# Start addresses of the on-chip operands of a 1-core transformer kernel: multiples of 128 bytes

## Chip, cores and metric

The kernel runs on 1 core of one Trainium2 chip. The metric is the device time of one execution in microseconds. TensorE has two clock levels, 1.2 and 2.4 GHz.

## What is computed

Three blocks one after the other on an activation `x` of 256 tokens by 1024 features, all in 4-byte floats. Each layer is a residual sum of feed-forward parts and one mixer:

```python
# first block, 2 layers (mixers: compressed/selected/window attention, then window attention)
x = x + 0.5 * swiglu(rmsnorm(x, ffn1_norm[i]), ffn1_w_gu[i], ffn1_w_down[i])   # D_FF = 2816
h = rmsnorm(x, mix_norm[i])
x = x + mixer(h)
x = x + 0.5 * swiglu(rmsnorm(x, ffn2_norm[i]), ffn2_w_gu[i], ffn2_w_down[i])
# second block, 1 layer: the same frame with shift, scale and gate made from c_2 @ w_ada_2
# third block, 4 layers (stick-breaking attention, short convolution, gated linear attention, stick-breaking)
h = h + rms_norm(m, norm_gains[i, 1])
f = jnp.square(jax.nn.relu(rms_norm(h, norm_gains[i, 2]) @ w_up)) @ w_down      # D_FF_3 = 4096
h = h + rms_norm(f, norm_gains[i, 3])
```

There are 6 gated feed-forward layers (silu) and 4 ReLU ones.

## The kernel before

**Split products.** Every large product is made of rounded operands (type F32R). A value is split into a rounded high part and the rest: ScalarE copies `raw` to `hi` (`split_hi`, L329), VectorE subtracts, `lo = raw - hi` (`split_lo`, L336). A product is then hi·hi + hi·lo + lo·hi, three matmuls added up in PSUM.

**Operands on chip.** Weights arrive in `ring_in` (units of 2048 columns, 1 MB) and `ring_down`, two slots each, and are split into `in_hi`, `in_lo` and `down_hi`, `down_lo`. Activations that enter a product lie transposed in `feat` (both parts in one tensor, `feat_hi` and `feat_lo`, 8 chunks of 256 tokens). Where a mixer's output projection comes just before, they lie in `feat2_hi` and `feat2_lo` instead, at the end of the arena (class `Feed`). The hidden values of a feed-forward unit are split into `hid_hi` and `hid_lo`; `act` holds them unsplit. `hyb_hi` and `hyb_lo` are activations of the second block's mixer.

**Feed-forward (class `FeedForward`).** TensorE turns over units: hidden(i), down(i-1), hidden(i+1), down(i). A unit of a gated layer is 128 gate and 128 up columns, 22 units; `_chunk` (L1099 to L1101) issues 16 x 3 matmuls of 256 columns, weights stationary and `feat` (or `feat2`) streamed. Its down projection (`_down_block`, L1169 to L1171) issues 4 x 3 matmuls of 512 columns, `hid` stationary, `down_hi` and `down_lo` streamed. A unit of a ReLU layer is 256 columns, 16 units; `_chunk` issues 16 pairs, one of 512 columns that streams `feat_hi` and `feat_lo` in two parts of 256 (L1097), one of 256 (L1098), and 24 down matmuls. ScalarE and VectorE split the next unit's weights meanwhile, and make the hidden values of this one.

**Mixer projections.** `Linear` (L1455 to L1457) and its kin (L4020 to L4022, L3816 to L3818) hold 128 tokens of features stationary and stream 512 columns of `in_hi` or `in_lo`. Others (L1985 to L1987, L3359 to L3361, L3996 to L3998) hold weights and stream 256 columns of `feat`. L1846 is a matmul of the stick-breaking attention on unsplit 4-byte operands of the arena.

**Modulation.** Three of the gated layers (the two `ffn1` and the second `ffn2` of the first block) have GpSimd work beside them that adds up `c_2 @ w_ada_2` from `mod_w` into `mod_sum`. The order on each engine is that of a list of stages; waits are semaphores written by hand.

**Placement.** `Core.__init__` allocates the tensors one after another, each from the current `nc.sbuf_base`. `ring_down`, `hid_hi` and `hid_lo` share the space of `proj`; `down_hi`, `down_lo`, `mod_sum`, `mod_w`, `feat2`, `hyb` and some masks share that of `arena`. The start bytes within a partition in the built program, and what is left over 128:

| tensor | before | over 128 | after | over 128 |
|---|---|---|---|---|
| const | 16512 | 0 | 16512 | 0 |
| x / y | 31584 / 39776 | 96 | same | 96 |
| feat | 47968 | 96 | 48000 | 0 |
| in_hi / in_lo / ring_in | 64352 / 80736 / 97120 | 96 | 64384 / 80768 / 97152 | 0 |
| act | 113504 | 96 | 113536 | 0 |
| proj, ring_down | 123040 | 32 | 123136 | 0 |
| hid_hi / hid_lo | 139424 / 143520 | 32 | 139520 / 143616 | 0 |
| arena, down_hi | 147744 | 32 | 147840 | 0 |
| down_lo | 164128 | 32 | 164224 | 0 |
| feat2_hi / feat2_lo | 205088 / 213280 | 32 | 205184 / 213376 | 0 |
| hyb_lo / hyb_hi | 199296 / 214304 | 0 / 32 | 199392 / 214400 | 96 / 0 |

Of the kernel before, what the change touches and what calls it, by code (L numbers as in the profile page):

```python
# [116 lines left out]
    return slice(n * BLK, (n + 1) * BLK)  # L117

class Signal:  # L120

# [15 lines left out]
class Core:  # L138

    def __init__(self, nc, ctx, dram):
        self.nc, self.dram = nc, dram

        def sb(name, *shape):
            return ctx.enter_context(nc.sbuf_tensor(name, [P, *shape], F32))
# [4 lines left out]
        def split(name, *shape):  # L150
            return ctx.enter_context(nc.sbuf_tensor(name, [P, *shape], F32R))

        self.sb, self.sig = sb, sig
        self.const = sb("const", CONST_N)
        self.cols = sb("cols", COL_N)
        self.x = sb("x", TT, D)
        self.y = sb("y", TT, D)

        self.feat = split("feat", 2, KC, TOKENS)
        self.feat_hi, self.feat_lo = self.feat[:, 0], self.feat[:, 1]  # L160
        self.in_hi = split("in_hi", RING, UNIT)
        self.in_lo = split("in_lo", RING, UNIT)
        self.ring_in = sb("ring_in", RING, UNIT)
# [3 lines left out]
        self.fold = sb("fold", TT, P)  # L167
        self.minus_half = sb("minus_half", 8)
        self.eps = sb("eps", 8)
        at = nc.sbuf_base  # L170
        self.proj = sb("proj", TT, PROJ_COLS)

        def placed(name, offset, dtype, *shape):
            return nc.alloc_sbuf_tensor_at(name, [P, *shape], dtype, offset=offset)
# [3 lines left out]
        self.hid_hi = placed("hid_hi", at, F32R, RING, 2 * TOKENS)  # L179
        at += 4 * RING * 2 * TOKENS  # L180
        self.hid_lo = placed("hid_lo", at, F32R, RING, 2 * TOKENS)
        at = nc.sbuf_base
        self.arena = sb("arena", ARENA)
        self.down_hi = placed("down_hi", at, F32R, RING, UNIT)
# [6 lines left out]
        at = nc.sbuf_base - 4 * 2 * KC * TOKENS  # L191
# [4332 lines left out]
```

## Time and profile before

| | |
|---|---|
| three timed runs, us | 2889.39, 2891.58, 2892.72 (median 2891.58) |
| profiled execution, span | 2889.2 us (the page gives this execution by its span alone) |
| busy: TensorE / VectorE / ScalarE / GpSimd | 96% / 66% / 42% / 21% |
| mean granted TensorE clock | 0.986 |
| DMA | 173 GB/s mean, 500 MB |

The busy share of an engine is the time in which some instruction of it runs. Matmuls are pipelined: the next one starts before the last has ended, so a matmul's printed duration isn't what it costs; the distance between two starts is. PE is TensorE, PEld its loading of stationary values, DVE is VectorE, ACT ScalarE, POOL GpSimd, SP the queue that issues DMAs. The names right of the arrow are the operands, the streamed one first, then the stationary one; `feat_hi` and `feat_lo` stand there for `feat2`, `feat` for both parts of `feat`. In `128*128 128x512`, the first is the rows and columns of the array that are used, the second the output.

### The profile page before, as it was taken

How to read it: one execution, taken by the hardware profiler on the slowest of the kernel's cores; microseconds unless marked ns; L12 is line 12 of the kernel's file. 1: busy time of each engine (PE TensorE's matmuls, PEld its weight loads, DVE VectorE, ACT ScalarE, POOL GpSimd, SP SyncE). 2: the span in 40 equal slices, each digit the busy share in tenths (PEclk: the TensorE clock that was granted, in tenths of full speed). 3: DMA queues.
4: the chain of work that ended last, by engine and by line, in shares of the span. 5: the costliest groups of instructions: out<-in, count | busy, mean ns of one | idle time of the engine just before them, and what ended most of it. 6: DMA issues, size and time to landing. Idle time of an engine off the chain costs nothing.

```text
span 2889.2 us, 43862 instructions
## 1 busy us (share of the span) xinstructions
PE 2775.3 (96%) x17408; PEld 2446.4 (85%) x17408; DVE 1903.6 (66%) x2046; ACT 1201.3 (42%) x1478; POOL 609.9 (21%) x510
## 2 busy tenths in 40 slices
PE   8999999999989999999899999999899989999998
PEld 7997789999878988988699897888788878888887
DVE  6985656688867885555655556666666657655665
ACT  4343443343444334334444345334433444435433
POOL 6953300068434861000100000000000320000000
PEclk9999999999999999999999999999999999999999
DMA  7745134557526664443355434544554345533542
GB/s 278 265 183 163 45 145 189 186 215 275 184 73 225 254 241 175 180 147 103 110 184 186 146 132 178 196 157 160 194 195 163 118 145 197 197 126 116 211 187 103
DMA packets 126466, 500.31 MB, mean 173 GB/s; under 512 B 11025, under 2 KB 12337, under 8 KB 92961
## 3 DMA queue, kind: packets, MB, share of 16 engines
q1 hardware_dynamic: 112768, 450.39, 42.8%
q0 software_dynamic: 13600, 48.60, 4.9%
q8 instruction: 65, 1.06, 0.2%
q14 instruction: 33, 0.26, 0.0%
HBM read 497.90 MB, written 1.05 MB: 173 GB/s over the span
## 4 chain that ended last, share of the span: by engine, by line
PE 74%; DVE 13%; issue 6%; ACT 3%; POOL 2%; DMA 1%; DVEq 0%; SPq 0%; ACTq 0%; POOLq 0%
PE duo L1097 7%; PE duo L1169 7%; PE duo L1170 7%; PE duo L1171 7%; PE duo L1099 6%; PE duo L1100 6%; PE duo L1101 6%; PE duo L1098 4%; DVE down_lo L336 3%; PE duo L1455 3%; PE duo L1457 3%; PE duo L1456 3%; DVE in_lo L336 3%; ACT in_hi L329 2%; DVE hid_hi L1279 1%
## 5 line engine op out<-in xcount | busy, mean ns | idle before, releaser
L336 DVE TENSOR_TENSOR in_lo<-ring_in,in_hi 128x2048 fp32r<-128x2048 f32 x296 | 706.5, 2387 | 306.1 <-ACT in_hi L329 305.9
L329 ACT CAST in_hi<-ring_in 128x2048 fp32r<-128x2048 f32 (+1 forms) x293 | 554.5, 1893 | 276.8 <-PE duo L1457 152.3
L1169 PE MATMUL duo<-down_hi,hid_hi 128*128 128x512 f32 x1040 | 412.4, 397 | 10.9 <-DVE hid_lo L1281 7.5
L1170 PE MATMUL duo<-down_lo,hid_hi 128*128 128x512 f32 x1040 | 409.7, 394 | 0.0
L1171 PE MATMUL duo<-down_hi,hid_lo 128*128 128x512 f32 x1040 | 409.5, 394 | 0.0
L1099 PE MATMUL duo<-feat,in_hi 128*128 128x256 f32 x1408 | 400.1, 284 | 6.5 <-DVE in_lo L336 6.1
L1100 PE MATMUL duo<-feat,in_hi 128*128 128x256 f32 x1408 | 399.3, 284 | 0.0
L1101 PE MATMUL duo<-feat,in_lo 128*128 128x256 f32 x1408 | 399.1, 283 | 0.0
L336 DVE TENSOR_TENSOR down_lo<-ring_down,down_hi 128x1024 fp32r<-128x1024 f32 (+1 forms) x196 | 373.1, 1904 | 34.4 <-ACT down_hi L329 34.4
L1097 PE MATMUL duo<-feat,in_hi 128*128 128x512 f32 x1024 | 360.4, 395 | 0.0
L329 ACT CAST down_hi<-ring_down 128x1024 fp32r<-128x1024 f32 (+1 forms) x196 | 260.2, 1328 | 73.3 <-PE duo L1171 72.1
L1098 PE MATMUL duo<-feat,in_lo 128*128 128x256 f32 x1024 | 284.3, 278 | 0.0
L1099 PEld LDWEIGHTS duo<-feat,in_hi 128*128 128x128 f32 x1408 | 270.5, 192 | 11.2 <-DVE in_lo L336 6.1
L1100 PEld LDWEIGHTS duo<-feat,in_hi 128*128 128x128 f32 x1408 | 270.9, 192 | 3.2
L1101 PEld LDWEIGHTS duo<-feat,in_lo 128*128 128x128 f32 x1408 | 270.8, 192 | 0.0
L1169 PEld LDWEIGHTS duo<-down_hi,hid_hi 128*128 128x128 f32 x1040 | 196.0, 188 | 55.8 <-issue 16.0
L1171 PEld LDWEIGHTS duo<-down_hi,hid_lo 128*128 128x128 f32 x1040 | 195.7, 188 | 45.8
L1097 PEld LDWEIGHTS duo<-feat,in_hi 128*128 128x128 f32 x1024 | 192.0, 188 | 45.6 <-DVE in_lo L336 0.5
L1170 PEld LDWEIGHTS duo<-down_lo,hid_hi 128*128 128x128 f32 x1040 | 196.1, 189 | 37.2
L908 POOL TENSOR_TENSOR small<-small,minus_half 128x1 f32<-128x1 f32 x16 | 8.9, 554 | 1024.6 <-DVE small L941 1024.3
L3122 POOL TENSOR_TENSOR mod_sum<-mod_sum,mod_w 128x1024 f32<-128x1024 f32 x63 | 210.1, 3335 | 5.3
L1219 ACT ACTIVATE act<-act 128x256 f32<-128x256 f32 x88 | 36.8, 418 | 416.9 <-DVE act L1269 416.9
(487 smaller groups left out, 5286.0 us busy)
## 6 DMA issues: line engine op xcount, KB each, us to landing
ring_in<-in_ffn_in SPq DMA_DIRECT2D x196, 1024.0 KB, 6.4
ring_down<-in_ffn_down SPq DMA_DIRECT2D x132, 512.0 KB, 3.5
ring_down<-in_ffn_down SPq DMA_DIRECT2D x64, 1024.0 KB, 4.8
mod_w<-in_w_ada POOLq DMA_DIRECT2D x72, 512.0 KB, 5.2
ring_in<-in_sb_w_qkv SPq DMA_DIRECT2D x24, 1024.0 KB, 5.1
ring_in<-in_conv_w_in SPq DMA_DIRECT2D x12, 1024.0 KB, 5.2
ring_in<-in_gla_w_in SPq DMA_DIRECT2D x12, 1024.0 KB, 5.1
ring_in<-in_nsa_w_in SPq DMA_DIRECT2D x10, 1024.0 KB, 5.3
```

What stands on the lines that cost most here:

```text
L329: act.copy(hi[:, s, 0:n], raw[:, s, 0:n]).then_inc(hi_ready.sem, 1)
L336: dve.tensor_tensor(lo[:, s, 0:n], raw[:, s, 0:n], hi[:, s, 0:n].bitcast(F32), ALU.subtract).then_inc(lo_ready.sem, 1)
L1097: pe.matmul(out.rearrange("p (s n) -> p s n", s=2), hi, k.feat[:, :, c, :], start=c == 0, stop=False, skip_group_check=True)
L1098: return pe.matmul(out[:, 0:TOKENS], lo, k.feat_hi[:, c, :], start=False, stop=(c == KC - 1), skip_group_check=True)
L1099: pe.matmul(out, hi, self.feat_hi[:, c, :], start=opens, stop=False, skip_group_check=True)
L1100: pe.matmul(out, hi, self.feat_lo[:, c, :], start=False, stop=False, skip_group_check=True)
L1101: return pe.matmul(out, lo, self.feat_hi[:, c, :], start=False, stop=(c == KC - 1), skip_group_check=True)
L1169: pe.matmul(out, k.hid_hi[:, j, rows], k.down_hi[:, s, cols], start=opens, stop=False)
L1170: pe.matmul(out, k.hid_hi[:, j, rows], k.down_lo[:, s, cols], start=False, stop=False)
L1171: return pe.matmul(out, k.hid_lo[:, j, rows], k.down_hi[:, s, cols], start=False, stop=closes)
L1455: pe.matmul(out, f_hi, w_hi[:, c, :], start=(h == 0 and c == 0), stop=False)
L3122: pool.tensor_tensor(total, total, mod.w[:, s, :], ALU.add).then_inc(mod.used.sem, 1)
```

## The change

Four constants of phases, all 0, and a helper that allocates a gap tensor up to the wanted phase. Two of the gaps exist in the built program (32 bytes before `feat`, 64 before `proj`); the other two are empty. Nothing else is touched: each engine issues the same instructions in the same order, with other addresses.

```diff
+LINE = 128
+FEATURE_PHASE, WEIGHT_PHASE, HIDDEN_PHASE, ARENA_PHASE = 0, 0, 0, 0
...
+        def phase(name, at):
+            gap = (at - nc.sbuf_base) % LINE
+            if gap:
+                sb(name, gap // 4)
...
+        phase("feature_gap", FEATURE_PHASE)
         self.feat = split("feat", 2, KC, TOKENS)
         self.feat_hi, self.feat_lo = self.feat[:, 0], self.feat[:, 1]
+        phase("weight_gap", WEIGHT_PHASE)
         self.in_hi = split("in_hi", RING, UNIT)
         self.in_lo = split("in_lo", RING, UNIT)
...
         self.eps = sb("eps", 8)
+        phase("hidden_gap", HIDDEN_PHASE)
         at = nc.sbuf_base
         self.proj = sb("proj", TT, PROJ_COLS)
...
         self.hid_lo = placed("hid_lo", at, F32R, RING, 2 * TOKENS)
+        phase("arena_gap", ARENA_PHASE)
         at = nc.sbuf_base
         self.arena = sb("arena", ARENA)
```

## Rows read from the trace of the kernel before

**Rows 1.** Page, sections 1 and 4: busy time per engine; the chain that ended last.

```profile
PE 2775.3 (96%) x17408; PEld 2446.4 (85%) x17408; DVE 1903.6 (66%) x2046; ACT 1201.3 (42%) x1478; POOL 609.9 (21%) x510
...
PE 74%; DVE 13%; issue 6%; ACT 3%; POOL 2%; DMA 1%; DVEq 0%; SPq 0%; ACTq 0%; POOLq 0%
```

**Rows 2.** Groups by line and form, TensorE: busy us, mean ns, idle before.

```profile
L1169 PE MATMUL duo<-down_hi,hid_hi 128*128 128x512 f32 x1040 | 412.4, 397 | 10.9 <-DVE hid_lo L1281 7.5 <-DVE hid_lo L1296 3.1
...
L1099 PE MATMUL duo<-feat,in_hi 128*128 128x256 f32 x1408 | 400.1, 284 | 6.5 <-DVE in_lo L336 6.1 <-DVE feat L615 0.5
...
L1097 PE MATMUL duo<-feat,in_hi 128*128 128x512 f32 x1024 | 360.4, 395 | 0.0
...
L1099 PE MATMUL duo<-feat_hi,in_hi 128*128 128x256 f32 x704 | 196.2, 279 | 0.1
...
L1455 PE MATMUL duo<-in_hi,feat 128*128 128x512 f32 x432 | 172.5, 399 | 3.7 <-DVE in_lo L336 3.6
...
L1985 PE MATMUL duo<-feat,in_hi 128*128 128x256 f32 x256 | 72.6, 284 | 0.0
```

**Rows 3.** Timeline, TensorE: start us, us, instruction; gated layer, `feat` streamed.

```profile
1479.75 0.28 PE L1099 MATMUL duo<-feat,in_hi 128*128 128x256 f32 x1
...
1481.43 0.28 PE L1101 MATMUL duo<-feat,in_lo 128*128 128x256 f32 x1
```

**Rows 4.** Timeline, TensorE; gated layer, `feat2_hi` and `feat2_lo` streamed.

```profile
449.65 0.28 PE L1099 MATMUL duo<-feat_hi,in_hi 128*128 128x256 f32 x1
...
451.69 0.28 PE L1099 MATMUL duo<-feat_hi,in_hi 128*128 128x256 f32 x1
```

**Rows 5.** Timeline, TensorE; down projection, split down weights streamed.

```profile
1490.43 0.40 PE L1169 MATMUL duo<-down_hi,hid_hi 128*128 128x512 f32 x1
...
1493.22 0.28 PE L1099 MATMUL duo<-feat,in_hi 128*128 128x256 f32 x1
```

**Rows 6.** Timeline, TensorE; ReLU layer, two-part stream, then one part.

```profile
1858.22 0.40 PE L1097 MATMUL duo<-feat,in_hi 128*128 128x512 f32 x1
...
1861.69 0.40 PE L1097 MATMUL duo<-feat,in_hi 128*128 128x512 f32 x1
```

**Rows 7.** Timeline, TensorE; mixer projection, `in_hi` and `in_lo` streamed.

```profile
252.26 0.40 PE L1455 MATMUL duo<-in_hi,feat 128*128 128x512 f32 x1
...
254.99 0.39 PE L1455 MATMUL duo<-in_hi,feat 128*128 128x512 f32 x1
```

**Rows 8.** Timeline, TensorE; before 22 us, the same stream as rows 3.

```profile
21.00 0.41 PE L1099 MATMUL duo<-feat,in_hi 128*128 128x256 f32 x1
...
21.64 0.41 PE L1099 MATMUL duo<-feat,in_hi 128*128 128x256 f32 x1
```

**Rows 9.** Timeline, and line L1846 alone: unsplit 4-byte operands.

```profile
1718.69 0.60 PE L1846 MATMUL duo<-arena,const 128*128 128x256 f32 x2
...
L1846 PE MATMUL duo<-arena,const x64: 378/379/483, 1708.1 to 2671.2; 128*128 128x256 f32 x64
```

**Rows 10.** Stretches of single layers: us, then each engine's busy us, clock, DMA.

```profile
53.20:206.60 153.40, 153.40 (x1073) 143.43 (x1071) 135.56 (x112) 58.64 (x55) 120.20 (x64) 1.00 0.66 244
...
920.90:1078.70 157.80, 152.50 (x1081) 141.18 (x1080) 138.81 (x114) 59.23 (x55) 123.23 (x66) 1.00 0.70 256
```

**Rows 11.** Waits of VectorE, 53.2 to 206.6 us: us in total, times, longest.

```profile
DVE act L1274 <- ACT act L1219: 8.7, 18, 0.5
DVE in_lo L336 <- ACT in_hi L329: 4.1, 5, 1.1
```

**Rows 12.** Timeline, TensorE; `in_hi`, `in_lo` streamed against `hyb_hi`, `hyb_lo`.

```profile
1407.28 0.39 PE L3816 MATMUL duo<-in_hi,hyb_hi 128*128 128x512 f32 x1
...
1409.34 0.39 PE L3816 MATMUL duo<-in_hi,hyb_hi 128*128 128x512 f32 x1
```

**Rows 13.** Groups of VectorE, 1824 to 1924 us (a ReLU layer).

```profile
L336 DVE TENSOR_TENSOR in_lo<-ring_in,in_hi 128x2048 fp32r<-128x2048 f32 x10 | 22.9, 2292 | 11.1 <-ACT in_hi L329 11.1
L336 DVE TENSOR_TENSOR down_lo<-ring_down,down_hi 128x2048 fp32r<-128x2048 f32 x9 | 20.6, 2292 | 6.1 <-ACT down_hi L329 6.1
```

## Prediction

> **What bounds the kernel now.** I read the page first. TensorE is busy 96% of the span, and the chain that ended last lies on it for 74% and on VectorE for 13% [rows 1]. So the kernel is bound by the rate of its matmuls, and a view of waits can tell little; next come the groups by line. Nearly all matmuls there are of the split kind (rounded 4-byte operands, three products for one), in few shapes: a stream of 512 or of 256 columns against 128x128 stationary values [rows 2]. The printed durations (about 395 and 280 ns) overlap, since matmuls are pipelined; what a matmul costs is the distance from its start to the next one's. That I take from the timeline, over many in a row.
>
> In a gated layer that streams `feat`, 14 steps take 1481.43 - 1479.75 = 1.68 us: 120.0 ns for 256 columns [rows 3]. In a gated layer that streams `feat2_hi` and `feat2_lo`, the same line with the same weight buffers, 18 steps take 2.04 us: 113.3 ns [rows 4]. At 2.4 GHz and one column a cycle it would be 106.7 ns. So the same shape has two prices, 13.3 and 6.7 ns above the ideal. What differs is where the stream starts: `feat` 96 bytes past a multiple of 128, `feat2` 32 bytes past one. The other streams are all off a multiple too. Down projection (32 past): 12 steps in 2.79 us, 232.5 ns for 512 columns, where the ideal is 213.3 [rows 5]. ReLU layer (96 past): 10 pairs of a 512- and a 256-column step in 3.47 us, 347 ns a pair against 320 [rows 6]. Mixer projection (96 past): 12 steps in 2.73 us, 227.5 ns [rows 7].
>
> **The change, part by part.** No instruction, wait or transfer is added, removed or reordered. From `feat` to `eps` everything moves up by 32 bytes, from `proj` on by 96. Every full-rate stream then starts on a multiple of 128, since its inner offsets are multiples of 512.
>
> The price of an aligned step lies between the ideal (106.7 and 213.3 ns) and today's 120 and 232 (above, should it get worse: the rival on the other side). I take 109 and 216: the ideal plus the 2 ns that the stream without visible excess shows [rows 9]. The terms:
> - ReLU layers, 4 with 16 units each. A unit has 16 pairs, (347 - 325) x 16 = 0.35 us, and 24 down steps, (232 - 216) x 24 = 0.38 us. 64 x 0.73 = **47 us**. They hold the 1024 steps of L1097 [rows 2]. VectorE waits there for ScalarE, and ScalarE for TensorE, so there is room [rows 13].
> - Gated layers without modulation work beside them that stream `feat`: 2 of 22 units. 48 steps x 11 ns + 12 x 16 ns = 0.72 us. 44 x 0.72 = **32 us**.
> - The one such layer that streams `feat2`: 48 x 4.3 + 12 x 16 = 0.40 us. 22 x 0.40 = **9 us**.
> - The three gated layers with modulation work on GpSimd (66 units) would give 40 us by TensorE alone. They won't. In the first, 18 units take 153.4 us, 8.52 each, and VectorE is busy for 135.6 of it, 7.53 each; to that come its waits for ScalarE, 8.7 + 4.1 us or 0.71 each, which lie inside a unit's own sequence [rows 10, 11]. VectorE thus can't turn a unit round in under about 8.2 us, where an aligned TensorE would want 7.8. In the third, 18 units take 157.8 us, 8.77 each, already more than TensorE's 48 x 0.113 + 12 x 0.232 = 8.2: it is paced by VectorE now [rows 10]. I take 0.2 us for the first's 22 units, 0.1 for the second's, none for the third's: **7 us**, between 0 and 30.
> - Mixer projections: 3 x 432 steps of 512 columns of L1455 to L1457 and 384 more in small groups, at 227 - 216 = 11 ns: 18 us. 3 x 256 steps of 256 columns of L1985 to L1987 and 576 more, at 11 ns: 15 us [rows 2, 7]. Between them TensorE waits for others now and then, so I count 85%: **28 us**.
> - The elementwise engines and the DMAs: nothing. VectorE's subtraction over 2048 elements takes 2292 ns both in the buffer 96 past and in the one 32 past, so it doesn't see the start [rows 13]; and transfers end ahead of need. Were each 2% faster it would show only in the three layers above, a few us.
>
> Sum: 47 + 32 + 9 + 7 + 28 = 123 us. The profiled execution has a span of 2889.2 us; 2889.2 - 123 = 2766. The median of the runs is 2.4 us above that span, so I forecast **2769 us**. With ideal prices the terms are 56, 38, 12, 30 and 41, 177 us in all, and the time 2714: the lower end.
>
> **The rivals.**
> - *Only part of the excess goes.* Rows 3 and 4 differ by 6.7 ns, one of two such steps. If the aligned start removes one step per matmul and the rest belongs to the change of stationary values, each step gains 6.7 ns: 64 x 56 x 6.7 = 24, 44 x 60 x 6.7 = 18, 22 x 60 x 6.7 = 9, modulation 7, mixers 3024 x 6.7 x 0.85 = 17; 75 us, time 2817. For it: 512 columns have an excess of 14 to 19 ns, no smaller than 256 columns, so it goes by matmul and not by column. Against it: rows 8 show no fixed cost of a matmul.
> - *The start has no effect.* The two prices of rows 3 and 4 would then come of something else, for instance of how far apart the two buffers lie. Time 2891.6. The Trainium skill, "SBUF — State Buffer", section "SBUF: two separate sides", has such a rule: SBUF lines of 16 bytes, with a penalty for each crossing. All starts here are multiples of 32 and so of 16 before and after, and by that rule nothing would change; the trace disagrees with it so far as it has two prices for one shape.
> - *Slower.* The price could go by where the stream and the stationary values start relative to each other: both 96 past costs 120.0 [rows 3], 64 bytes apart costs 113.3 [rows 4]. The change puts everything on one start. Then nothing of the rest moves, since those pairs are equal already, and the `feat2` layers pay what `feat` pays: 22 x 48 x 6.7 = 7 us in the open layer and up to as much in the modulation layer, 7 to 14 us, time about 2901. It decides if equal starts collide at all. Against it: with `in_hi` 96 past streamed against `hyb` values at 32 and 0 past, nine steps take 2.06 us, 228.9 ns, not less than the 227.5 of equal starts [rows 7, 12]. The Trainium skill, same page, section "Who interferes with whom", gives TensorE two independent read ports for the two operands, which speaks against it too; no run here shows the ports.
>
> **How the numbers follow.** The forecast has 0.58 (its own range 2714 to 2800, whose width is the unknown price and the modulation layers), partial gain 0.22 (2800 to 2850, with a tail), no effect 0.11, slower 0.09. About 0.2% or 6 us is what a measurement tells from no change. So faster 0.80, same 0.11, slower 0.09. The two last make the 2 in 10 that the range may leave out: 2714 to 2860, the upper end where under a third of the gain comes.
>
> **What would show it.** Right: rows 3 at 107 to 110 ns a step, and rows 4 the same, so that `feat` and `feat2` have one price; rows 5 and 7 at 213 to 217; a pair of rows 6 at 320 to 327. Rows 8 and 9 stay. In the modulation layers new waits of TensorE for VectorE's `hid_lo`, and units of 8.2 us or more. Wrong: 113 ns in rows 3 and 4 means the partial rival, unchanged distances the second, `feat2` at 120 the third. If distances fall as said and the time doesn't, the waits of TensorE for VectorE would tell where VectorE had been the pace all along.

## The result and the profile after

The changed kernel takes 2905.05 us (median of 9 runs, 2898.96 to 2907.41); before, 2895.0 us (median of 9 runs, 2889.39 to 2898.83). The ratio is 1.0038, interval 1.0027 to 1.0048: slower by 0.4%, 10 to 11 us. The forecast was 2769 us.

The page of the changed kernel, sections 1 and 4, against rows 1:

```profile
PE 2793.8 (96%) x17408; PEld 2464.5 (85%) x17408; DVE 1906.1 (66%) x2046; ACT 1200.9 (41%) x1478; POOL 610.1 (21%) x510
...
PE 75%; DVE 13%; issue 5%; ACT 3%; POOL 2%; DMA 2%; DVEq 0%; SPq 0%; ACTq 0%; POOLq 0%
```

TensorE's share is as it was. It is busy 18.5 us longer, which covers the 16.2 us of longer span. So the question is the distance of the starts again. The lines are 13 further down in this kernel: L1112 is L1099, L1110 is L1097, L1182 is L1169, L1468 is L1455. The timeline of TensorE, a gated layer that streams `feat`, against rows 3:

```profile
1488.00 0.28 PE L1112 MATMUL duo<-feat,in_hi 128*128 128x256 f32 x1
...
1490.88 0.28 PE L1112 MATMUL duo<-feat,in_hi 128*128 128x256 f32 x1
```

24 steps in 2.88 us, 120.0 ns, as before. A gated layer that streams `feat2`, against rows 4:

```profile
457.75 0.28 PE L1113 MATMUL duo<-feat_lo,in_hi 128*128 128x256 f32 x1
...
458.95 0.28 PE L1114 MATMUL duo<-feat_hi,in_lo 128*128 128x256 f32 x1
```

10 steps in 1.20 us, 120 ns, where it was 113.3. A down projection, against rows 5, 11 steps in 2.55 us, 232 ns, as before:

```profile
1475.27 0.39 PE L1182 MATMUL duo<-down_hi,hid_hi 128*128 128x512 f32 x1
...
1477.82 0.39 PE L1184 MATMUL duo<-down_hi,hid_lo 128*128 128x512 f32 x1
```

A ReLU layer, against rows 6, 9 pairs in 3.18 us, 353 ns, where it was 347:

```profile
1847.71 0.40 PE L1110 MATMUL duo<-feat,in_hi 128*128 128x512 f32 x1
...
1850.89 0.40 PE L1110 MATMUL duo<-feat,in_hi 128*128 128x512 f32 x1
```

A mixer projection, against rows 7, 9 steps in 2.04 us, 226.7 ns, as before:

```profile
259.38 0.39 PE L1468 MATMUL duo<-in_hi,feat 128*128 128x512 f32 x1
...
261.42 0.39 PE L1468 MATMUL duo<-in_hi,feat 128*128 128x512 f32 x1
```

No step came near the forecast price, and two became dearer. Adding up the distances of all starts on the lines concerned, waits included, gives 253.9 us before and 259.9 after for the `feat2` layers (+6.0: +5.5 in the layer without modulation work, +0.5 in the other), and 364.9 and 369.9 for the ReLU layers (+5.0); the gated `feat` layers +2.0, at unchanged steps, and the down steps -1.6. Together that is 11.4 us, where the medians differ by 10.

The two profiled executions are 16.2 us apart, not 10. Their mean granted clocks account for most of the rest; the first row is of the changed kernel, the second of the one before:

```profile
core 0: 2905.4 us, clock 0.984
```

```profile
core 0: 2889.2 us, clock 0.986
```

2905.4 x 0.016 less 2889.2 x 0.014 is 6 us, an estimate that takes TensorE for the pace all along. One place is early; one stretch of the changed kernel (busy us per engine, granted clock, DMA):

```profile
243.60:257.10 13.50, 13.50 (x57) 12.73 (x57) 3.31 (x10) 0.30 (x1) 0.00 (x0) 0.50 0.25 78
```

It is 13.5 us at 0.50, the lower level, during a run of 64 matmuls of 75 strided columns (L2378) and the first projection steps behind it; before, those 64 matmuls ran at 1.00, in 8.2 us where they took 12.0 here. The nine executions of the changed kernel have means of 0.984 to 0.986, and 22 executions of the kernel before, measured along with the first four kernels below, 0.982 to 0.987, with the same mean of 0.985, so the clock isn't the reason for the 10 us.

### The profile page after: what moved, and what is told of

It is laid out like the page before. It is cut to its first block, busy times and chain, and to the rows that moved or that the text cites. A ratio compares the mean times of both kernels' runs of the same rounds, so it can differ in the third digit from the quotient of the medians.

```text
span 2905.4 us, 43862 instructions
## 1 busy us (share of the span) xinstructions
PE 2793.8 (96%) x17408; PEld 2464.5 (85%) x17408; DVE 1906.1 (66%) x2046; ACT 1200.9 (41%) x1478; POOL 610.1 (21%) x510
## 4 chain that ended last, share of the span: by engine, by line
PE 75%; DVE 13%; issue 5%; ACT 3%; POOL 2%; DMA 2%; DVEq 0%; SPq 0%; ACTq 0%; POOLq 0%
PE duo L1110 7%; PE duo L1182 7%; PE duo L1184 7%; PE duo L1183 7%; PE duo L1112 6%; PE duo L1114 6%; PE duo L1113 6%; PE duo L1111 4%; PE duo L1468 3%; PE duo L1469 3%; PE duo L1470 3%; DVE down_lo L349 3%; DVE in_lo L349 2%; ACT in_hi L342 2%; DVE hid_hi L1292 1%
## 5 line engine op out<-in xcount | busy, mean ns | idle before, releaser
L1182 PE MATMUL duo<-down_hi,hid_hi 128*128 128x512 f32 x1040 | 410.9, 395 | 9.0 <-DVE hid_lo L1294 5.6
L1112 PE MATMUL duo<-feat,in_hi 128*128 128x256 f32 x1408 | 400.1, 284 | 6.2 <-DVE in_lo L349 5.7
L1110 PE MATMUL duo<-feat,in_hi 128*128 128x512 f32 x1024 | 365.3, 399 | 0.0
L1112 PEld LDWEIGHTS duo<-feat,in_hi 128*128 128x128 f32 x1408 | 271.1, 193 | 10.7 <-DVE in_lo L349 6.1
L1182 PEld LDWEIGHTS duo<-down_hi,hid_hi 128*128 128x128 f32 x1040 | 196.5, 189 | 53.5 <-issue 13.2
L1110 PEld LDWEIGHTS duo<-feat,in_hi 128*128 128x128 f32 x1024 | 192.3, 188 | 48.0 <-DVE in_lo L349 0.6
```

What stands on the lines that cost most here:

```text
L1110: pe.matmul(out.rearrange("p (s n) -> p s n", s=2), hi, k.feat[:, :, c, :], start=c == 0, stop=False, skip_group_check=True)
L1112: pe.matmul(out, hi, self.feat_hi[:, c, :], start=opens, stop=False, skip_group_check=True)
L1182: pe.matmul(out, k.hid_hi[:, j, rows], k.down_hi[:, s, cols], start=opens, stop=False)
```

## The experiments

After the result, two theories stood against each other. **Relative start:** the price of a step goes by the distance between the start of the streamed and of the stationary operand. **Own start:** it goes by the streamed operand's place, with 32 past a multiple of 128 cheap for a reason of its own. All kernels but the two of TensorE alone are the changed one with other constants or with gaps left out; f, a and h stand for the starts of `feat` (or `feat2`), the down weights and `hid`, counted from `in_hi` modulo 256. Before they are f 0 (`feat2` 192), a 192, h 64; in the changed kernel f 0 (`feat2` 0), a 0, h 128. A down step's own distance, stream against stationary, is a less h: 128 in both.

### Four placements

```diff
-FEATURE_PHASE, WEIGHT_PHASE, HIDDEN_PHASE, ARENA_PHASE = 0, 0, 0, 0
+FEATURE_PHASE, WEIGHT_PHASE, HIDDEN_PHASE, ARENA_PHASE = 64, 0, 0, 0       # feat64
+FEATURE_PHASE, WEIGHT_PHASE, HIDDEN_PHASE, ARENA_PHASE = 32, 32, 32, 32    # all32
+FEATURE_PHASE, WEIGHT_PHASE, HIDDEN_PHASE, ARENA_PHASE = 0, 0, 0, 64       # arena64
+FEATURE_PHASE, WEIGHT_PHASE, HIDDEN_PHASE, ARENA_PHASE = 32, 0, 0, 32      # feat32arena32
```

> The changed kernel with one constant other: feat starts 64 past a multiple of 128, all else on multiples. Theory 1 (what counts is how far apart, modulo 128 bytes, the streamed and the stationary operand start; 64 apart is cheap, equal is dear): a 256-column step of feat against in_hi falls from 120 to 113.3 ns, the feat2 layers stay at 120; 4224 + 1344 such steps save 6.7 ns each, 37 us, less some 8 us where VectorE paces: 2870 to 2880 us. Theory 2 (what counts is the streamed operand's own start, 32 past being cheap): no change known for 64, and equal to the changed kernel, about 2905 us, if only 32 is cheap.

> The changed kernel with all four starts 32 past a multiple of 128, so still equal to each other. Theory 1 (relative start): as the changed kernel, 120 ns for feat and for feat2 against in_hi, 2900 to 2910 us. Theory 2 (the stream's own start, 32 is cheap): both fall to 113.3 ns, about 45 us less, 2860 us.

> The changed kernel with the arena alone 64 past a multiple of 128: feat2 and down_hi, down_lo start 64 past, hid_hi and hid_lo and in_hi on multiples. Theory 1 (relative start): feat2 steps back to 113.3 ns, and the down steps (512 columns, today 231.5 ns) fall by some 7 ns, 3120 x 7 = 22 us; with feat2's 10 us, 2870 to 2880. Theory 2 (own start): neither, 2905, or a change of both that does not depend on the partner.

> The changed kernel with feat and the arena 32 past a multiple of 128, in_hi and hid on multiples: streams and stationary operands 32 apart. Theory 1: a price between that of 0 apart (120 ns) and that of 64 apart (113.3) or equal to one of them; it shows which distances count. Theory 2: 113.3 ns for feat and feat2, since both start 32 past, about 2860 us.

Medians and ratios to the kernel before (2894.47 us on this chip; the changed kernel's row is from the first measurement, against 2895.0), and mean distances between starts that I worked out from each trace, stalls left out (gated and down in ns a step, ReLU in ns a pair):

| | us | ratio, interval | gated, `feat` | gated, `feat2` | down | ReLU pair |
|---|---|---|---|---|---|---|
| before | 2894.47 | | 120.5 | 115.2 | 232.0 | 347 |
| changed | 2905.05 | 1.0038 (1.0027 to 1.0048) | 120.7 | 120.2 | 231.6 | 352 |
| feat64 | 2896.19 | 0.9999 (0.9990 to 1.0009) | 116.4 | 120.2 | 232.0 | 352 |
| all32 | 2904.39 | 1.0045 (1.0029 to 1.0061) | 120.4 | 120.3 | 231.7 | 352 |
| arena64 | 2905.38 | 1.0034 (1.0018 to 1.0049) | 120.8 | 118.2 | 233.2 | 350 |
| feat32arena32 | 2903.95 | 1.0031 (1.0018 to 1.0043) | 119.4 | 117.3 | 234.1 | 347 |

In bytes modulo 256, stream less stationary, `all32` has the distances of the changed kernel; `feat64` differs from it in `feat` (192), `arena64` in `feat2` (64) and the down steps (192), `feat32arena32` in `feat` (160), `feat2` (32) and the down steps (160).

`all32` decides: streams that start 32 past, as the cheap one did before, cost 120 once their partner starts there too. Own start falls. But relative start, as I had it, missed numbers: the times of `feat64` and `arena64`, both expected at 2870 to 2880, were 2896 and 2905; 64 apart costs 116.4 in one place and 118.2 in the other, and down steps got dearer, not cheaper, as they moved apart. The addresses show that the two places are 192 and 64 apart modulo 256. And the ReLU pair has two prices at one distance; in `arena64` two whole layers have 347 and two 352.

The mean of 116.4 isn't a price either. Two neighbouring units of `feat64`, in one layer, with the same placement and the same down steps between them: 45 steps in 5.30 us and in 5.11 us, 117.8 and 113.6 ns.

```profile
1475.23 0.28 PE L1112 MATMUL duo<-feat,in_hi 128*128 128x256 f32 x1
...
1480.53 0.28 PE L1112 MATMUL duo<-feat,in_hi 128*128 128x256 f32 x1
```

```profile
1483.65 0.28 PE L1112 MATMUL duo<-feat,in_hi 128*128 128x256 f32 x1
...
1488.76 0.28 PE L1112 MATMUL duo<-feat,in_hi 128*128 128x256 f32 x1
```

Of its 80 gated `feat` units that run in one piece, 41 are at 113.3 and 39 at 117.8, and in the two layers without modulation work the two take turns. The kernel before has both prices too: of 40 such `feat2` units 31 are at 113.3, as in rows 4, and 9 at 117.8, which makes its mean of 115.2.

### The prices alone

TensorE alone, in the kernel's pattern: two steps on the weights' high part, one on the low part, 48 steps per placement.

> Leaves out the whole computation: TensorE alone issues runs of 48 split-style steps (weights hi, hi, lo stationary, 256 or 512 columns streamed) for many pairs of start offsets, nothing else runs. Relative-start theory: the step depends on stream start minus stationary start only, alike for stationary at 0, 32, 64, 96 and 128 past; 120 ns at 0 apart, 113 to 118 at 32, 64 and 192 apart, by distance modulo 256 rather than 128 (the full kernel had 113.3 at 192 and 118 at 64 apart), repeating at 512, 1024, 2048. Own-start theory: it changes with the stream's start at equal distance. If the excess belongs to the matmul and not to placement at all, every pair has the same price, 120 ns. Against length: an excess per matmul stays near 13 ns from 128 to 512 columns; one per line grows with the length.

The timeline of this run, one line of the pattern (every third matmul). Stream and weights both at 0, then both at 96: 33 steps in 3.96 and 3.97 us, 120.0 and 120.3 ns.

```profile
50.01 0.28 PE L65 MATMUL acc<-big 128*128 128x256 f32 x1
...
53.97 0.28 PE L65 MATMUL acc<-big 128*128 128x256 f32 x1
```

```profile
220.81 0.28 PE L65 MATMUL acc<-big 128*128 128x256 f32 x1
...
224.78 0.28 PE L65 MATMUL acc<-big 128*128 128x256 f32 x1
```

Weights at 32, stream at 96, so 64 apart: 27 steps in 3.18 us, 117.8 ns.

```profile
181.75 0.28 PE L65 MATMUL acc<-big 128*128 128x256 f32 x1
...
184.93 0.28 PE L65 MATMUL acc<-big 128*128 128x256 f32 x1
```

Weights at 32, stream at 224, so 192 apart: 30 steps in 3.40 us, 113.3 ns.

```profile
193.06 0.28 PE L65 MATMUL acc<-big 128*128 128x256 f32 x1
...
196.46 0.28 PE L65 MATMUL acc<-big 128*128 128x256 f32 x1
```

And 512 columns, 0 apart and 128 apart: 33 steps in 7.48 and 7.69 us, 226.7 and 233.0 ns.

```profile
420.85 0.39 PE L81 MATMUL acc<-big 128*128 128x512 f32 x1
...
428.33 0.39 PE L81 MATMUL acc<-big 128*128 128x512 f32 x1
```

```profile
465.18 0.39 PE L81 MATMUL acc<-big 128*128 128x512 f32 x1
...
472.87 0.40 PE L81 MATMUL acc<-big 128*128 128x512 f32 x1
```

The table of this run, worked out in the same way over the last 36 distances of each placement, stationary at 0:

| stream minus stationary, bytes | 0 | 32 | 64 | 96 | 128 | 160 | 192 | 224 | 256 |
|---|---|---|---|---|---|---|---|---|---|
| 256 columns, ns | 120.0 | 117.8 | 117.8 | 120.0 | 118.6 | 118.6 | 117.8 or 113.3 | 118.3 | 120.0 |
| 512 columns, ns | 226.7 | 233.3 | 228.9 | 233.3 | 233.3 | 234.2 | 233.3 | 233.3 | |

With the stationary operand at 32, 64, 96 and 128 the price at 0 was 120.0, at 64 apart 117.8 and at 128 apart 118.7, each time; 256 to 480 repeated 0 to 224, and 512, 1024 and 2048 cost what 0 costs. So the distance counts, modulo 256, and the own start doesn't. Three points more. No placement reaches the ideal. 512 columns want the opposite of 256: 0 apart is their best, where 256 columns have, with 96 apart, the worst of these places. And 192 apart has two prices: 117.8 in the sweep with weights at 0, where steps 160 apart ran just before; 113.3 with weights at 32, 64, 96 and 128, where steps 128 apart did; and 113.3 with weights at 0 too when every step used the high part.

At distance 0, 320 columns took 146.7 ns, 384 took 173.3 and 512 took 226.7, each 13.3 above one column a cycle, as 256 do; 448 took 206.7, 20 above. So at this distance the excess belongs to the step, not to the columns. It isn't so everywhere: at distance 192 it grows, 320 columns 146.7 ns, 384 174.7, 448 202.2 and 512 233.3. Nor below 256 columns: at the upper clock 96 and 192 columns both took about 112 ns a step, and at the lower level, to which the granted clock fell during these short steps, 96, 128 and 192 columns all took 213.3, what 256 columns take there.

### The two halves of the change

```diff
         # featgap: the 32 bytes before feat alone
-        phase("hidden_gap", HIDDEN_PHASE)
-        phase("arena_gap", ARENA_PHASE)
         # hidgap: 64 bytes before proj alone
-        phase("feature_gap", FEATURE_PHASE)
-        phase("weight_gap", WEIGHT_PHASE)
-        phase("hidden_gap", HIDDEN_PHASE)
+        sb("hidden_gap", 16)
-        phase("arena_gap", ARENA_PHASE)
```

> Half the change: only the 32-byte gap before feat, so everything from feat on moves up by 32 bytes and keeps its distance to everything else there. Relative-start theory: feat2 stays 192 from in_hi modulo 256 and keeps 113.3 ns, no product changes its price, and the time is that of the kernel before, within 0.2%. Own-start theory: feat and in_hi on multiples of 128 now cost what they cost in the changed kernel.

> The other half: only the 64-byte gap before proj, nothing on a multiple of 128 that was not before. Relative-start theory: feat2 comes to 0 from in_hi, its 256-column steps go from 113.3 to 120 ns as in the changed kernel, 22 x 48 x 6.7 = 7 us in the open layer and up to 7 in the modulation layer: 0.25% to 0.45% slower than before. Own-start theory: no such step, as before.

`featgap` 2893.61 us against 2893.77, ratio 0.9992 (0.9981 to 1.0003). `hidgap` 2901.13, ratio 1.0029 (1.0017 to 1.0041). The timeline of the `feat2` layer in `featgap`, 21 steps in 2.38 us, 113.3 ns, with `in_hi` on a multiple of 128:

```profile
469.92 0.28 PE L1110 MATMUL duo<-feat_hi,in_hi 128*128 128x256 f32 x1
...
472.30 0.28 PE L1110 MATMUL duo<-feat_hi,in_hi 128*128 128x256 f32 x1
```

and in `hidgap`, 21 steps in 2.51 us, 120 ns, with nothing newly aligned:

```profile
457.14 0.28 PE L1109 MATMUL duo<-feat_hi,in_hi 128*128 128x256 f32 x1
...
459.65 0.28 PE L1109 MATMUL duo<-feat_hi,in_hi 128*128 128x256 f32 x1
```

The alignment of `feat` and `in_hi` does nothing that can be told from no change; the 64 bytes before `proj` carry the loss, as far as the intervals tell. They move `feat2` from 192 to 0 from `in_hi`. The ReLU pairs went with them: 347 in `featgap`, 352 in `hidgap`, though `feat` kept its distance to `in_hi` in both.

### Two placements built from the prices

```diff
-LINE = 128
+LINE = 256
-FEATURE_PHASE, WEIGHT_PHASE, HIDDEN_PHASE, ARENA_PHASE = 0, 0, 0, 0
+FEATURE_PHASE, WEIGHT_PHASE, HIDDEN_PHASE, ARENA_PHASE = 128, 128, 0, 0    # down0
+FEATURE_PHASE, WEIGHT_PHASE, HIDDEN_PHASE, ARENA_PHASE = 192, 0, 192, 192  # rel192
```

> The changed kernel with the arena 128 bytes further, so that down_hi, down_lo start 0 from hid_hi, hid_lo modulo 256 in place of 128. Relative-start theory, by the prices run: 512-column down steps fall from 231.7 to 226.7 ns, 3120 x 5 = 15.6 us less; feat2 is then 128 from in_hi, 118.7 in place of 120 ns. About 2888 us, 0.5% faster than the changed kernel. If down steps keep 231 ns, the price is not the relation's but comes of the other engines or of PSUM.

> A version made from the prices run: feat and feat2 192 from in_hi, down weights 0 from hid, modulo 256. Relative-start theory: 256-column gated and mixer steps at 113.3 to 117.8 ns for feat as for feat2, down steps 226.7, mixer projections of 512 columns 228.9 in place of 226.7 (a loss of 3 us). About 15.6 (down) + 37 x 0.4 to 0.9 (feat) - 3 us less, cut where VectorE paces: 2865 to 2880 us, 0.5% to 1% faster than before. If the time falls by under 0.3%, VectorE or the ReLU layers took the rest.

`down0` 2896.21 us, ratio 1.0007 (0.9997 to 1.0017): 0.3% less than the changed kernel where 0.5% was expected. Down steps fell to a mean of 228.2 ns, not 226.7, and `feat2` stayed at 120.5, though it now lay 128 from `in_hi`, where `prices` has 118.6: that distance has a dearer price as well. `rel192` 2887.85 us, ratio 0.9977 (0.9966 to 0.9988): faster than before, but short of the 2865 to 2880 expected. Its gated steps, on `feat2` here, were in the dearer of the two patterns, 21 steps in 2.48 us, 118 ns:

```profile
469.96 0.28 PE L1112 MATMUL duo<-feat_hi,in_hi 128*128 128x256 f32 x1
...
472.44 0.28 PE L1112 MATMUL duo<-feat_hi,in_hi 128*128 128x256 f32 x1
```

### What decides between two prices

Two prices at one distance could come of the other engines, or of the down steps that run between the gated ones. So TensorE alone again, in the kernel's own alternation, with f at 0 or 192 and all a and h in steps of 64.

> Leaves out the whole computation: TensorE alone, in the kernel's own alternation (48 gated steps and 12 down steps, or 16 ReLU pairs and 24 down steps), with feat 0 or 192 from in_hi and the down weights and hid at 0, 64, 128 or 192 from it. The full kernels had two prices for one distance: ReLU pairs 347 ns before and 352 ns after at feat 0 from in_hi in both, gated steps at 192 either 113.3 or 117.8. Theory A (the pairs settle into one of several patterns, and the run of down steps ahead decides which): the same two prices come back here, 347 where the down weights are at 192 and hid at 64 (as before), 352 at 0 and 128 (as after); gated steps at 192 take 113.3 entered from (192, 64) and 117.8 from (192, 192). Theory B (the other engines' reads and writes of the on-chip memory make the second price): here each distance has one price whatever the down steps are.

Each placement runs two units, one unit being the gated or ReLU steps and then the down steps; the price of a placement is read from its second unit, which is entered from its own down steps. The timeline of this run, gated steps at f 192, entered from down steps at (a, h) = (192, 64), as before's `feat2` layer, and at (192, 192), as in `rel192`: 39 steps in 4.44 and 4.59 us, 113.8 and 117.7 ns.

```profile
549.39 0.28 PE L60 MATMUL acc<-big 128*128 128x256 f32 x1
...
553.83 0.28 PE L60 MATMUL acc<-big 128*128 128x256 f32 x1
```

```profile
582.24 0.28 PE L60 MATMUL acc<-big 128*128 128x256 f32 x1
...
586.83 0.28 PE L60 MATMUL acc<-big 128*128 128x256 f32 x1
```

ReLU pairs at f 0, entered from (192, 64), as before, and from (0, 0): 14 pairs in 4.85 us, 346.4 ns, and 13 pairs in 4.59 us, 353.1 ns.

```profile
891.84 0.40 PE L70 MATMUL acc<-big 128*128 128x512 f32 x1
...
896.69 0.40 PE L70 MATMUL acc<-big 128*128 128x512 f32 x1
```

```profile
601.99 0.40 PE L70 MATMUL acc<-big 128*128 128x512 f32 x1
...
606.58 0.40 PE L70 MATMUL acc<-big 128*128 128x512 f32 x1
```

No other engine runs here, and both prices are there. Over the 16 placements at f 192 the gated steps took 113.3 or 113.4 in seven and 117.8 in nine, nothing else; ReLU pairs at f 0 took 346.4 to 346.7 in nine and 352.6 to 353.7 in seven. So the other engines aren't needed for it, and Theory A holds so far. One placement missed: (0, 128), the changed kernel's, gave a ReLU pair of 346.4 here and 352 in the full kernels.

The first units of the placements, entered from the down steps of the placement ahead, show more. Gated units at f 192, both entered from down steps at (0, 64): 45 steps in 5.11 and 5.30 us, 113.6 and 117.8 ns.

```profile
348.76 0.28 PE L60 MATMUL acc<-big 128*128 128x256 f32 x1
...
353.87 0.28 PE L60 MATMUL acc<-big 128*128 128x256 f32 x1
```

```profile
357.00 0.28 PE L60 MATMUL acc<-big 128*128 128x256 f32 x1
...
362.30 0.28 PE L60 MATMUL acc<-big 128*128 128x256 f32 x1
```

What differs is the gated unit ahead of those down steps: 117.8 ns ahead of the first, 113.3 ahead of the second. (0, 128), the placement of `feat64`, gave gated steps of 113.3 and 117.8 ns in the same way, which is the alternation of `feat64`. For ReLU pairs (0, 128) gave 346.4 and then 353.6, though the pairs ahead took about 346.5 both times; so the miss is no contradiction, and the price of the unit ahead doesn't settle it either. Most placements gave one price both times. With 117.8 ns in the gated unit ahead, (0, 0) led to 117.8 and (0, 64) to 113.3. So the down steps take part in the choice, and alone they don't settle it: what ran before them counts too. Whether something that this run doesn't copy counts besides, such as the distances between the high and low parts' buffers, is not shown.

The least whole unit at f 192 was (192, 128), 8.20 us against 8.53 for f 0 and 8.25 for f 192 with (192, 64). Two kernels test that, one good and one middling by these units:

```diff
+LINE = 256
+FEATURE_PHASE, WEIGHT_PHASE, HIDDEN_PHASE, ARENA_PHASE = 192, 0, 128, 192  # hid128
+FEATURE_PHASE, WEIGHT_PHASE, HIDDEN_PHASE, ARENA_PHASE = 192, 0, 64, 192   # hid64
```

> The placement with the least time in the run of alternations: feat, feat2 and the down weights 192 from in_hi, hid 128 from it (modulo 256). There a gated unit takes 8.20 us against 8.53 for before's placement with feat and 8.25 with feat2, a ReLU unit 11.16 against 11.11. 44 x 0.33 + 22 x 0.05 - 64 x 0.05 = 12 us less, some 4 to 7 in the mixers' 256-column steps, 3 more in their 512-column steps, a few less where VectorE paces: about 15 us, 0.4% to 0.7% faster than before, and gated steps at 113.3 ns for feat and feat2 alike. Had rel192's 117.8 been the other engines' doing, they would stay at 117.8 here.

> As hid128, but hid 64 from in_hi, as before: the alternations give 8.25 us for a gated unit and 11.21 for a ReLU unit. 44 x 0.28 - 64 x 0.09 = 6.5 us less, mixers 4 less, so 0.2% to 0.5% faster than before, behind hid128 by some 5 us; ReLU pairs at 353 ns, gated steps at 113.3.

`hid128` 2874.13 us against 2892.9, ratio **0.9935** (0.9921 to 0.9950). `hid64` 2883.07, ratio 0.9964 (0.9952 to 0.9976). Both in the order that the units gave, 19 and 10 us less where some 15 and 10 were expected; `hid128` beats both kernels of the study. 68 of its 80 gated `feat` units are at 113.3 ns, the other 12 at 117.8, and its ReLU pairs are at 353, dearer than before's 347. Its down steps are 64 apart, where before's are 128, and took a mean of 229.5 ns against 232.0. From one unit's first step to the next's in the gated `feat` layer, `hid128` and then before, 8.20 and 8.53 us, to the hundredth what the alternation gave:

```profile
1475.72 0.28 PE L1112 MATMUL duo<-feat,in_hi 128*128 128x256 f32 x1
...
1483.92 0.28 PE L1112 MATMUL duo<-feat,in_hi 128*128 128x256 f32 x1
```

```profile
1476.16 0.28 PE L1099 MATMUL duo<-feat,in_hi 128*128 128x256 f32 x1
...
1484.69 0.28 PE L1099 MATMUL duo<-feat,in_hi 128*128 128x256 f32 x1
```

Section 1 of its page, against rows 1, 25.6 us less of TensorE:

```profile
PE 2749.7 (96%) x17408; PEld 2419.1 (84%) x17408; DVE 1907.5 (66%) x2046; ACT 1201.1 (42%) x1478; POOL 609.8 (21%) x510
```

Not all of it reaches the end: the span of this execution is 16.6 us shorter. The waits of TensorE for `hid_lo`, `hid128` and then before (us in total, times, longest):

```profile
PE duo L1182 <- DVE hid_lo L1294: 17.2, 18, 2.1
```

```profile
PE duo L1169 <- DVE hid_lo L1281: 7.5, 9, 1.7
```

These waits alone grew by 9.7 us, in the layers that VectorE paces, which is about what is missing.

## Why the prediction was wrong

**The premise.** "That fits an extra fetch for the partly used ends of a run of bytes, which an aligned start would spare." This step failed. `prices` has the same 120 ns at 0 past as at 32, 64, 96 and 128 past when the partner moves along, and `featgap` has the alignment of `feat` and `in_hi` without a gain. The two prices of rows 3 and 4, 120.0 and 113.3, were real, and they were the whole evidence; I read them as 96 past against 32 past, when they were 0 apart against 192 apart. The rows differed in both, and I named the one.

**The price of an aligned step**, 109 and 216 ns, is nowhere; measured 120 and 232. With it fall the terms of 47, 32, 9 and 28 us. The `feat2` term had the wrong sign: of the 9 us forecast for the `feat2` layer without modulation work about half was to come from the gated steps; the distances there grew by 5.5 us.

**Rows 8 and 9.** At the lower clock there is no excess. The 2 ns taken from rows 9 were a misreading: 0.60 less 0.379 is 0.221 us, 7 ns above 213.3 by rounded figures, and over all such pairs of L1846 the trace has a mean of 217.7 ns, 4 above. The rows still say that most of the excess belongs to full rate. They don't say that the start makes it, and I let them count for that.

**The modulation layers.** The term of 7 us fell with the rest, but its reason stands: in `hid128`, where TensorE did become faster, its waits for VectorE's `hid_lo` went from 7.5 to 17.2 us.

**The rivals.** The slower one named the mechanism ("the change puts everything on one start", and "the `feat2` layers pay what `feat` pays") and came out at 2901, 9 us above the median known then, where the measured difference is 10; I had given it 0.09. That its 7 to 14 us for the `feat2` layers (measured 6.0) met the whole difference is in part luck, since 5 us of it are the ReLU layers'. Some of its parts were off. It had the distance modulo 128, where 256 counts, so it took the down steps for equal starts; they are 128 apart before and after. And it had nothing for the ReLU layers, +5 us, which changed pattern at unchanged distance. The 64 bytes apart that it named for rows 4 are 192 modulo 256; steps 64 apart cost 117.8. What I held against it, 228.9 ns apart to 227.5 together (rows 7, 12), was true for 512 columns and has the opposite sign for 256; I tested a rule for one length on the other. The Trainium skill, "SBUF — State Buffer", section "Who interferes with whom", gives TensorE two independent read ports; the trace disagrees at full rate so far as one operand's address changes the price of a stream of the other, 120.0 against 113.3 ns. The partial rival is out, as nothing gained; its sum also let the `feat2` steps gain 6.7 ns, which its own sign, 113 ns in rows 4, rules out. The one without effect is out as stated. For the latter I had cited lines of 16 bytes from the same page (they stand in its section "Specifications (TRN2)"): here 16 bytes more between stream and weights changed a step from 120.0 to 116.7 ns in `prices`, so what matters is not crossing such lines alone.

**Not settled:** why distance matters and what fixes the pattern. It was shown that two prices exist with TensorE alone, and that both the down steps ahead and what ran before them take part in the choice; why the ReLU pairs of the changed kernel stay at 352 is open, and the distance between high and low parts wasn't varied.

## What to carry over

When two rows of one shape have two prices, list everything in which they differ before giving one of them as the cause; here a kernel of TensorE alone, without any of the computation, sorted out in one run what four full placements could not. For full-rate 4-byte matmuls place operands relative to each other: the start modulo 256 bytes of the stream against the stationary operand is worth up to 6% of a 256-column step (a placement at 192 can fall back to 117.8 ns, 2%), while starting both on multiples of 128 brought nothing. And measure the alternation as the program runs it, over several units, since the steps ahead decide part of the price.

## What the runs showed that I had not expected

- The price of a 256-column step goes by the distance of its two operands modulo 256 bytes, from 113.3 to 120.0 ns in steps of 32 bytes, where the ideal is 106.7 (4 bytes apart cost 123.3, 16 bytes 116.7); for 512 columns from 226.7 to 234.2, with 0 apart the best.
- At one distance a run of 48 steps holds one of two prices (113.3 or 117.8; 347 or 353 a ReLU pair), with TensorE alone as in the full kernel. Some placements keep one price unit after unit, and in others it changes from unit to unit with the same matmuls ahead, as in `feat64`.
- A stream of 96 or 192 columns costs about as much a step as one of 256: 112 ns at the upper clock level, 213.3 at the lower.
- A kernel with the same instructions in the same order ranged from 0.9935 to 1.0045 of the time before by its gaps of up to 192 bytes.
